# The row of a norm's factors: through a small table in HBM instead of products and a copy

## What is computed

```python
def _rms(x, gain):
    x32 = x.astype(jnp.float32)
    y = x32 * lax.rsqrt(jnp.mean(x32 * x32, axis=-1, keepdims=True) + RMS_EPS)
    return (y * gain.astype(jnp.float32)).astype(x.dtype)

def _swiglu(xn, w_in, w_out):
    a, b = jnp.split(xn @ w_in, 2, axis=-1)
    return (jax.nn.silu(a) * b) @ w_out
...
        h = x + 0.5 * _swiglu(_rms(x, ffn1_norm[i]), ffn1_w_in[i], ffn1_w_out[i])
```

## Time and profile before

| | |
|---|---|
| device time, three runs | 1404.26, 1405.69, 1405.73 us; median 1405.69 |
| profiled execution, first to last instruction (span) | 1402.8 us |
| PE busy | 1393.1 us, 99% of the span |
| DVE busy | 912.6 us, 65% |
| ACT busy | 738.2 us, 53% |
| POOL busy | 94.9 us, 7% |
| data moved by DMA | 248.88 MB, mean 177 GB/s |

### The profile page before, as it was taken

The page is one execution under the profiler, slowest core; times in us unless marked ns, Lnnn a source line. Parts: engine busy times, 40 slices in busy tenths (PEclk is TensorE's granted clock), DMA queues, the critical chain, the costliest instruction groups (busy, mean ns, idle before and its releaser), DMA issues.

```text
span 1402.8 us, 21585 instructions
## 1 busy us (share of the span) xinstructions
PE 1393.1 (99%) x7935; PEld 1195.5 (85%) x7935; DVE 912.6 (65%) x1114; ACT 738.2 (53%) x973; POOL 94.9 (7%) x111
## 2 busy tenths in 40 slices
PE   9999999999999999999999999999999999999999
PEld 8888888888888888888888888888888888888887
DVE  5666666787666676666755455766667867676664
ACT  6544565666454565445544454644546755454442
POOL 0000022310000000000000110000001051100000
PEclk9999999999999999999999999999999999999999
DMA  7665655426565556656655445555656432165552
GB/s 256 222 195 179 209 197 180 140 91 209 181 196 192 180 180 188 199 183 194 230 191 188 153 154 166 191 199 180 197 191 220 132 109 92 61 210 200 190 188 83
DMA packets 156460, 248.88 MB, mean 177 GB/s; under 512 B 9728, under 2 KB 101488, under 8 KB 156144
## 3 DMA queue, kind: packets, MB, share of 16 engines
q1 hardware_dynamic: 153728, 243.54, 53.1%
q10 hardware_dynamic: 2672, 4.51, 0.9%
HBM read 246.97 MB, written 1.05 MB: 177 GB/s over the span
## 4 chain that ended last, share of the span: by engine, by line
PE 96%; DVE 2%; ACT 1%; DMA 0%; issue 0%; SPq 0%; ACTq 0%; DVEq 0%
PE bank L1982 30%; PE bank L1991 16%; PE bank L1907 14%; PE bank L1909 14%; PE bank L1908 14%; PE bank L1924 1%; PE bank L2357 1%; DVE w_lo L1290 1%; ACT w_hi L590 1%; DMA x<-in_x 0%; PE bank L2002 0%; PE bank L2300 0%; PE bank L2422 0%; PE bank L2153 0%; PE bank L2276 0%
## 5 line engine op out<-in xcount | busy, mean ns | idle before, releaser
L1290 DVE TENSOR_TENSOR w_lo<-raw,w_hi 128x2048 fp32r<-128x2048 f32 x225 | 514.8, 2292 | 325.5 <-ACT w_hi L590 325.1
L590 ACT ACTIVATE w_hi<-raw 128x2048 fp32r<-128x2048 f32 x228 | 434.5, 1909 | 208.0 <-PE bank L1991 143.2
L1982 PE MATMUL bank<-xT,w_hi 128*128 128x512 f32 x1860 | 444.6, 391 | 0.0
L1982 PEld LDWEIGHTS bank<-xT,w_hi 128*128 128x128 f32 x1860 | 344.0, 188 | 67.9
L1991 PEld LDWEIGHTS bank<-xT,w_lo 128*128 128x128 f32 x1824 | 226.6, 192 | 4.6
L1991 PE MATMUL bank<-xT,w_lo 128*128 128x256 f32 x1824 | 228.3, 283 | 0.0
L1909 PE MATMUL bank<-w_hi,hT_lo 128*128 128x512 f32 x500 | 194.8, 390 | 0.0
L1907 PE MATMUL bank<-w_hi,hT_hi 128*128 128x512 f32 x496 | 193.6, 390 | 0.0
L1908 PE MATMUL bank<-w_lo,hT_hi 128*128 128x512 f32 x496 | 193.1, 389 | 0.0
L1907 PE MATMUL bank<-w_hi,xT 128*128 128x512 f32 x396 | 157.4, 397 | 0.0
L1909 PE MATMUL bank<-w_hi,xT 128*128 128x512 f32 x396 | 154.6, 390 | 0.0
(11 more groups left out here) (343 smaller groups left out, 1066.0 us busy)
## 6 DMA issues: line engine op xcount, KB each, us to landing
raw<-in_ffn_w_in SPq DMA_DIRECT2D x174, 512.0 KB, 4.7
raw<-in_ffn_w_out SPq DMA_DIRECT2D x88, 512.0 KB, 4.2
raw<-in_w_ff SPq DMA_DIRECT2D x64, 512.0 KB, 4.3
raw<-in_rt_w_in SPq DMA_DIRECT2D x48, 512.0 KB, 4.5
raw<-in_w_in SPq DMA_DIRECT2D x28, 512.0 KB, 4.6
raw<-in_da_w_in SPq DMA_DIRECT2D x24, 512.0 KB, 4.6
raw<-in_rt_w_out SPq DMA_DIRECT2D x16, 512.0 KB, 4.1
raw<-in_da_w_out SPq DMA_DIRECT2D x8, 512.0 KB, 4.1
```

What stands on the lines that cost most here:

```text
L590: act.activation(w_hi[:, n % RING, :], raw[:, n % RING, :], ACT.Copy).then_inc(hi_ready, 1)
L1290: dve.tensor_tensor(w_lo[:, n % RING, :], raw[:, n % RING, :], w_hi[:, n % RING, :].bitcast(F32), ALU.subtract).then_inc(lo_ready, 1)
L1982: mm = pe.matmul(bank[at + b][:, :], hi[:, k, b * P:b * P + P], flat(xT[:, 4 * j + k, :, :]), start=j == 0 and k == 0, stop=j == 1 and k == 3)
```

## The change

The two products, the copy out of the bank and PE's wait for it are gone. After a norm's `rstd` is there, ACT issues a transfer of it to row r of a table `rstd_rows` of 5 by 256 float32 in HBM (`send_row`: 128 pieces of two numbers, so that the factor of token t*128+p lands at position 2p+t). One weight split later ACT waits for that transfer's completion and issues a second one, from the table to `rstd_row` on all partitions (`fetch_row`: the same 1 KB for each of 128 partitions, 128 KB). The row is now in the order p, t; DVE's multiplications read it with `by_token`, in steps of two elements. The semaphore `row_ready` counts in sixteens, as transfers do. PE's first chunk in ffn0 still waits for the second part of the gains.

```diff
         scale_ready = sem("scale_ready")
-        row_psum = sem("row_psum")
+        row_sent = sem("row_sent")
         row_ready = sem("row_ready")
...
+        def by_token(row, k):
+
+            return row.rearrange("p (n t) -> p t n", t=2).unsqueeze(1).to_broadcast([P, k, 2, P])
+
         def by_four(ap):
...
             eng.wait_ge(wt_used, RING + n + 1 + RING * turns)
+
+        rstd_rows = nc.dram_tensor("rstd_rows", (5, T), F32, kind="Internal").ap()
...
-            def norm(g, n=None):
+            def send_row(r, g):
+
+                act.wait_ge(rstd_ready, g + 1)
+                act.dma_start(rstd_rows[r].rearrange("(p t) -> p t", t=2), rstd[:, :]).then_inc(row_sent, 16)
+
+            def fetch_row(r, dst):
+
+                act.wait_ge(row_sent, 16 * (r + 1))
+                act.dma_start(dst, rstd_rows[r].partition_broadcast(P)).then_inc(row_ready, 16)
+
+            def norm(g, n=None, row=None):
...
                 hi(1)
+                if row is not None:
+                    send_row(row, g)
                 split(n + 2)
...
-                def row():
-                    act.wait_ge(row_psum, f + 1)
-                    act.activation(rstd_row, bank[4][:, 0:T], ACT.Copy).then_inc(row_ready, 1)
-
                 if f == 0:
                     split(n0 + 2)
+                    send_row(0, 0)
                 split(n0 + 3)
-                row()
+                fetch_row(f, rstd_row)
                 silu(0, at=0)
...
                     .then_inc(mx_bias, 16)
-                norm(6, n0)
+                norm(6, n0, row=4)
                 act.wait_ge(gain_psum, 2)
...
                 split(n0 + 3)
-                act.wait_ge(row_psum, 5)
-                act.activation(mx_row, bank[4][:, 0:T], ACT.Copy).then_inc(row_ready, 1)
+                fetch_row(4, mx_row)
                 cross(0)
...
             da()
-            norm(2, first["ffn1"])
+            norm(2, first["ffn1"], row=1)
             ffn(1, first["ffn1"])
-            norm(3, first["ffn2"])
+            norm(3, first["ffn2"], row=2)
             ffn(2, first["ffn2"])
             rt()
-            norm(5, first["ffn3"])
+            norm(5, first["ffn3"], row=3)
             ffn(3, first["ffn3"])
...
                     if at == 0:
-                        dve.wait_ge(row_ready, f + 1)
+                        dve.wait_ge(row_ready, 16 * (f + 1))
                     dve.wait_ge(in_taken, done + 2)
-                    both = relu[:, 1, :].rearrange("p (k n) -> p k n", k=2)
-                    dve.tensor_tensor(both, both, rstd_row.unsqueeze(1).to_broadcast([P, 2, T]), ALU.mult)\
+                    both = relu[:, 1, :].rearrange("p (k t n) -> p k t n", k=2, t=2)
+                    dve.tensor_tensor(both, both, by_token(rstd_row, 2), ALU.mult)\
                         .then_inc(gate_ready, 1)
...
                     if m == 0:
-                        dve.wait_ge(row_ready, 5)
-                    taken = conv_in[:, 4 * m:4 * m + 4, 3:3 + T]
-                    dve.tensor_tensor(taken, taken, mx_row.unsqueeze(1).to_broadcast([P, 4, T]), ALU.mult)\
+                        dve.wait_ge(row_ready, 16 * 5)
+                    taken = conv_in[:, 4 * m:4 * m + 4, 3:3 + T].rearrange("p k (t n) -> p k t n", t=2)
+                    dve.tensor_tensor(taken, taken, by_token(mx_row, 4), ALU.mult)\
                         .then_inc(mx_conv_in, 1)
...
-            def whole_block(n, j, at, turns=0, norm=None, free=None, row=None):
+            def whole_block(n, j, at, turns=0, norm=None, free=None):
...
                             mm.then_inc(in_done, 1)
-                        if row is not None and b == 0:
-                            pe.wait_ge(gain_ready, 2)
-                            pe.wait_ge(rstd_ready, norm + 1)
-                            for t in range(2):
-                                tr = pe.matmul(bank[4][:, t * P:t * P + P], rstd[:, t:t + 1].to_broadcast([P, P]), ident,
-                                               start=t == 0, stop=t == 1)
-                            tr.then_inc(row_psum, 1)
                 mm.then_inc(wt_used, 1)
...
                     whole_block(n0, 0, 0, norm=g)
-                whole_block(n0 + 1, 1, 0, norm=g, row=True)
+                whole_block(n0 + 1, 1, 0, norm=g)
                 def chunk(c, i, start):
-                    if start:
-                        pe.wait_ge(row_ready, f + 1)
+                    if start and f == 0:
+                        pe.wait_ge(gain_ready, 2)
                     whole_block(n0 + 2, 0, 4, turns=i, free=None if start else 4 * WHOLE[f] + 4 * i)
...
                 for m in range(3):
-                    if m == 1:
-                        pe.wait_ge(row_ready, 5)
-                    elif m == 2:
+                    if m == 2:
                         pe.wait_ge(mx_convw, 1)
...
                         pe.transpose(bank[0][:, 0:48], conv_row, ident[0:48, 0:48]).then_inc(mx_convw_psum, 1)
-                    whole_block(n0 + 2 * m + 1, 1, m % 2 * 4, norm=6 if m == 0 else None, row=True if m == 0 else None)
+                    whole_block(n0 + 2 * m + 1, 1, m % 2 * 4, norm=6 if m == 0 else None)
                 for m in range(3, 7):
                         if m == 3 and j == 0:

```

## The result

| | before | after |
| --- | --- | --- |
| median of 6 runs each, same chip, us | 1405.31 (1404.26 to 1405.78) | 1414.57 (1412.95 to 1422.35) |
| ratio of the means, 95% interval | | 1.0074 [1.0062, 1.0087] |
| span of the profiled execution, us | 1402.8 | 1414.1 |
| mean granted clock of that execution | 0.999 | 0.997 |

The change costs 9.3 us where 2.15 us of gain were forecast. The six runs of the change differ by more than those of before, and the longest has the lowest mean granted clock: 1422.35 us at 0.993, the others 1412.95 to 1415.92 at 0.997 or 0.998.

The account below looks back on a forecast made before the run. PE, with 96% of the chain that ended last, was taken as the bound. Removed products -2.45 us plus a 0.3 us loss at ffn0 gave -2.15, so 1405.69 became 1403.5 us, range 1401.8 to 1405.8.

Parts of the forecast that it names:

- The products: On PE at five norms: removing each row's products saves 0.49 us, 2.45 us in all, all on the chain.
- DVE's step of two: DVE's multiplications by the row, read at every second number, stay at 692 ns; rival of twice as slow, 1404.2 us, chance 0.12.
- The slack: Before PE needs the first out_block's split: 0.77 us at ffn0, 2.61 at ffn1 to ffn3, 2.36 in the mixer.
- What do the two transfers take?: Write to HBM plus copy to 128 partitions: 5.1 to 9.2 us; 0.3 us late at ffn0, hidden elsewhere.
- only two weight loads to share: At ffn1 the DMA engines have just two weight loads to share, argued against the row coming late everywhere.
- the row comes too late everywhere: 8-byte writes slow under weight loads delay the row at all places; at a 12 us pair, 1412.4 us; chance 0.08.
- its formula: With L for the pair, loss is L - 7.6 at ffn0 and three times L - 10.4 at the others.
- the loss of 3.2 at ffn0 alone: Late end at ffn0: first transfer lands at 24.4, second takes 5.4, row at 29.8 against a limit of 26.61.
- The rival on the products' price: PE's product pairs cost 0.61 us each instead of 0.49, saving 3.05 us: 1402.6 us; chance 0.2.

Follow-up runs that it names:

- e12: Kernel before without the products and without transfers; one constant row loaded once, behind the gains, multiplies everywhere: 1402.62 us, ratio 0.9983.
- e9: The change, but the second transfer reads an input's row instead of the table's, still waiting for the first: 1412.29 us in one run.
- e2: The change without the first transfer; the second reads an input's row and waits for nothing: 1402.68 us, ratio 0.9985.
- e5: The change with two waits on SP, holding weight loads until the first transfer has landed and until the row is there: 1403.75 us, ratio 0.9991.
- e8: Kernel before plus five kinds of small transfer after its last store, three times each; its time, some 35 to 60 us above before, means nothing.
- e11: The change with only the second chunk's weight loads held until the row is there; w_out still loads beside the first transfer: 1408.7 us in one run.
- e4: The change, but the second transfer reads 128 different rows of an input instead of the table's row: 1413.18 us in one run.
- e6: The change with ACT and DVE splitting the second weight matrix's block ahead of the turn, at every chunk: 1410.61 us, ratio 1.0043.

## Why the prediction was wrong

- **The products** (2.45 us): right. 2.3 measured (e12), and the pieces join, as forecast: the 32 products of the mixer's norm take 7.28 us in one piece, with the change and in e12, where they took 0.93 + 0.45 + 6.39 = 7.77 before. That is 0.49 again.
- **DVE's step of two**: right. 44 multiplications at 692 ns, as the earlier trace rows, and 1.23 us in the mixer, as the earlier trace rows.
- **The slack**: right at the feed-forwards in place, size and order (7.6 and 10.4 us, by which pairs of 14.0, 12.8, 12.2 and 12.0 would lose 6.4 + 2.4 + 1.8 + 1.6). PE waited 5.85 + 1.82 + 1.37 + 1.11, which is 0.4 to 0.6 us less at each, of which 0.24 at each comes back behind the wait. Wrong in the mixer: I gave it 2.36 us of slack, yet with the row there 13.9 us after the first issue PE waited for nothing. The stretch of 32 products that I took for the start of the late block begins with 16 of the block before it, so half of it, 3.6 us of slack, was not counted.
- **"What do the two transfers take?"** is the step that failed. I priced the pair at 5.1 to 9.2 us by the landings of the earlier trace rows (7.9 at ffn0), and it took 12.0 to 14.0: 5.3 to 7.1 us for the write and 6.4 to 7.0 for the copy. Every row that I took (the lambdas, an output quarter, a q gain) was a landing at another moment, and I went from operation to operation, not from moment to moment. e9 against e2 shows the same read at 5.9 and 3.0 us; e5 and e8 show the write at 2.5 to 3.2 without loads just ahead, against 5.3 to 7.1 with them; e11 shows the copy alone at 3.9 to 4.5. The trace of before did show the loads: at ffn1 SP issues `w_out` at 316.19, when `rstd` is written, and four `w_in` loads at 321.88. I counted "only two weight loads to share" and saw bandwidth; what counted is what was issued within about a microsecond. Yet the nearest rows of the trace of before would not have given the 12 us either: in the mixer three small loads of 24, 64 and 256 KB, issued 1.2 to 2.1 us behind SP's first load of 1063.44, took 4.1, 4.1 and 4.3 us, and two of those are past ffn0's 7.6 but inside 10.4.
- **The rival "the row comes too late everywhere"** is what happened, with the mechanism, the places and, at L = 12, the time: 1412.4 forecast, 1414.57 measured. At the measured times of the pair its formula gives 12.2 - 2.45 = 9.75 us, against 9.3; that this is so close is partly luck, since the waits were 2.05 us smaller than by the formula, and the clock and the first products behind the waits took 2.5 that it has not. It had a chance of 0.08, because "no small transfer in the trace is over 5.3 us". Here the ends of the range themselves were taken from the wrong moment, and so the range of 1401.8 to 1405.8 missed. It had also been drawn inside its own terms: the loss of 3.2 at ffn0 alone gave 1406.4.
- **The clock** was in no case: 1.5 us at ffn0, on top of a wait of 5.85.
- **The rival on the products' price** (0.61 each, 1402.6): the trace speaks against it, with 7.77 against 7.28 us for the stretch. The runs' times do not tell: e12's interval of 1.1 to 3.7 us holds both 2.45 and 3.05.

The Trainium skill had a line that I did not weigh: "DMA: Bandwidth & Descriptors", Latency and other measured facts, gives the access latency of HBM as 0.2 us on average and 2 us at high load. The runs show more than that: 2.6 to 3.0 us at the medians for the table's row, the write and the input's row beside the loads, against the quiet, and 4.3 for e4's different rows (6.5 against 2.2); whether it is that latency they do not show.

What stays open: why loads issued just ahead on another queue delay a small transfer by 2 to 4 us. The DMA engines' mean busy share at ffn1 was 0.59 over the first transfer (325.3 to 330.8), with 0.92 in its first 2.2 us and nothing in its last 1.1, and 0.77 over the second (330.84 to 337.84), so full DMA engines for the whole time are not the answer. Nor does the mean share tell a slow read from a quick one well: 0.77 over e9's 6.2 us at ffn1, but still 0.61 over e2's 2.9. The runs show only that it happens, and that it is gone, or nearly, when the loads are held back (e5 for the write, e11 for the copy).

## What to carry to other kernels

Price a new transfer by the moment at which it will be issued: look in the trace for what other queues issue within the microsecond ahead and beside it, and take as its bound the landing of something small beside such loads, or measure it. A chain of two dependent transfers pays that twice. Where a stage has slack for it and the loads beside it can be held back by two waits, the trade won here what four rows' products cost PE (2.0 us of 1405); where a stage has little slack, as the first one here with 0.77 us, leave the work on the engine.

## What the runs showed of the hardware

- The same 128 KB copy of an input row to 128 partitions: 2.9 us in the quiet (e8), issued between loads 2.9 to 3.0 at ffn1 to ffn3 and 4.1 to 4.2 at ffn0 and in the mixer (e2), 5.9 right behind 512 KB loads (e9).
- In the quiet, a 1 KB write to HBM in 8-byte pieces takes 2.7 us and a 64 KB write in 512-byte pieces 1.5. Reading back one row of 1 KB that was just written, for 128 partitions, takes 4.0 (e11, without loads beside it: 3.9 to 4.5), an input's row 2.9, and 128 different rows 2.2.
- After 5.85 us of idling PE's granted clock was 0.56 over the next 4 us, and products came every 0.43 us instead of 0.23 until it returned, six of them (after). e6, with 3.3 us of idling, shows twelve such. In e11, with 2.41 us, they came every 0.23 to 0.33 us at first, and every 0.43 us from 39.98 to 42.96, beginning 1.1 us after PE had started again. After e5's 0.60 us there was no such loss (1.00 over the first 50 us).
